# Hybrid decoder layer with grouped experts: expert slots padded to 32 rows instead of 128, four experts side by side in TensorE's column groups

## The reference, cut to what matters

```python
g_idx = jnp.argmax(g_logits, axis=-1)                      # 4 groups
top_v, top_i = lax.top_k(e_sel, 2)                         # 2 of the group's 4 experts
top_w = jax.nn.softmax(top_v, axis=-1) * p_g
combine = ...                                              # (tokens, 16), two entries per token
hg = jnp.einsum('td,edf->tef', t, w_e_gate)                # d 1024, f 256
hu = jnp.einsum('td,edf->tef', t, w_e_up)
act = jax.nn.silu(hg) * hu * combine[:, :, None]
return jnp.einsum('tef,efd->td', act, w_e_down)
```

## Time and profile before

| | |
|---|---|
| median of 3 runs | 1389.41 us |
| the profiled execution: span | 1389.9 us |
| TensorE matmul busy | 1280.3 us (92%) |
| VectorE busy | 1003.6 us (72%) |
| ScalarE busy | 742.2 us (53%) |
| mean granted TensorE clock | 0.967 |
| DMA moved | 229.41 MB, mean 165 GB/s |

### The profile page before, as it was taken

One profiled execution on the slowest core, in us unless ns is written; L12 is line 12 of the kernel. 1 busy time (PEld: TensorE's weight loads), 2 busy tenths in 40 slices (PEclk: granted clock), 3 DMA queues, 4 the chain that ended last, 5 costly groups with the idle time before them and its releaser, 6 DMA issues.

```text
span 1389.9 us, 25529 instructions
## 1 busy us (share of the span) xinstructions
PE 1280.3 (92%) x9230; PEld 1108.9 (80%) x9230; DVE 1003.6 (72%) x1532; ACT 742.2 (53%) x1323; POOL 129.9 (9%) x95
## 2 busy tenths in 40 slices
PE   4799999999999999999999996999389999999966
PEld 3598999999999999999999984777278887888832
DVE  2534457677585875858758667699879998999948
ACT  1445334454454544545545555422348998999825
POOL 1533200000000000000000000000011111111042
PEclk9899999999999999999999998999669999999988
DMA  9887433332342333322333243563177989655876
GB/s 321 261 277 243 134 106 102 88 84 84 88 117 66 89 95 94 115 59 82 107 97 102 84 138 91 163 199 152 76 280 254 372 292 376 205 184 182 285 258 200
DMA packets 210855, 229.41 MB, mean 165 GB/s; under 512 B 17942, under 2 KB 184666, under 8 KB 210619
## 3 DMA queue, kind: packets, MB, share of 16 engines
q1 hardware_dynamic: 195499, 173.33, 39.8%
q0 software_dynamic: 6976, 25.23, 5.4%
q10 hardware_dynamic: 8280, 29.51, 5.4%
HBM read 173.00 MB, written 46.79 MB: 158 GB/s over the span
## 4 chain that ended last, share of the span: by engine, by line
PE 72%; DVE 12%; DMA 4%; ACT 4%; SPq 3%; issue 3%; POOL 1%; ACTq 0%; DVEq 0%; POOLq 0%
PE AB L993 11%; PE AB L997 11%; PE AB L994 11%; PE S L918 6%; PE S L920 6%; PE S L919 6%; PE S L1093 4%; PE T L1119 3%; ACT F L1500 2%; DMA F<-in_b_ada 2%; PE OB L918 2%; PE OB L919 1%; PE OB L920 1%; SPq L624 1%; ACT R L1500 1%
## 5 line engine op out<-in xcount | busy, mean ns | idle before, releaser
L1500 ACT ACTIVATE R<-F 128x1024 fp32r<-128x1024 f32 (+4 forms) x306 | 292.4, 1003 | 74.2 <-DVE F L2084 39.6
L993 PE MATMUL AB<-R 128*128 128x344 f32 x960 | 314.9, 332 | 1.2 <-ACT F L1500 1.2
L994 PE MATMUL AB<-R 128*128 128x344 f32 x960 | 303.7, 320 | 0.0
L918 PE MATMUL S<-R 128*128 128x512 f32 x480 | 192.3, 401 | 2.0 <-ACT F L1500 1.6
L920 PE MATMUL S<-R 128*128 128x512 f32 x480 | 187.8, 391 | 0.0
L919 PE MATMUL S<-R 128*128 128x512 f32 x480 | 187.4, 390 | 0.0
L993 PEld LDWEIGHTS AB<-R 128*128 128x128 f32 x960 | 181.1, 189 | 4.8 <-issue 4.6
L994 PEld LDWEIGHTS AB<-R 128*128 128x128 f32 x960 | 181.4, 189 | 1.7 <-issue 1.7
L997 PE MATMUL AB<-R 128*128 128x344 f32 x960 | 171.6, 320 | 0.0
L1500 ACT ACTIVATE F<-AB 128x344 f32<-128x344 f32 (+3 forms) x129 | 59.0, 460 | 208.9 <-PE AB L997 193.5
L997 PEld LDWEIGHTS AB<-R 128*128 128x128 f32 x960 | 155.5, 188 | 0.0
(11 more groups left out here) (297 smaller groups left out, 2260.2 us busy)
## 6 DMA issues: line engine op xcount, KB each, us to landing
F<-in_w_ada SPq DMA_DIRECT2D x24, 1024.0 KB
F<-in_w_in SPq DMA_DIRECT2D x44, 512.0 KB, 4.2
F<-in_w_e_gate SPq DMA_DIRECT2D x16, 1024.0 KB, 5.9
F<-in_w_e_up SPq DMA_DIRECT2D x16, 1024.0 KB, 10.7
F<-in_w_e_down SPq DMA_DIRECT2D x16, 1024.0 KB, 10.9
y_d<-F ACTq DMA_DIRECT2D x32, 512.0 KB, 7.4
out<-F SPq DMA_DIRECT2D x24, 512.0 KB, 4.0
F<-F SPq DMA_DIRECT2D x192, 43.0 KB, 1.9
```

Of the source, the lines that this page charges most:

```text
L918: mm(out, w[0], m[1], start=start, stop=False)
L993: mm(bank[:, 0:PIECE], whl[b][0][:, k, :], x[1][:, k, :], start=(k == 0), stop=False)
L994: mm(bank[:, 0:PIECE], whl[b][0][:, k, :], x[0][:, k, :], start=False, stop=False)
L1500: return nc.scalar.activation(out, in_, func, **kw)
```

## The change

Slots are padded to 32 rows. 2064 pairs then take at most 80 subtiles of 32, laid out as four lanes of 20: lane j holds subtiles 20 j to 20 j + 19, in the order of the experts. A step n takes subtile n of each lane, four subtiles of up to four experts; the rows of lane j are rows 32 j to 32 j + 31 of the step's tile. There are 20 steps. The high and low splits are gone, of weights and of rows: products are native fp32 with the weights as they landed, each with a stationary operand of 32 columns whose output goes to 32 partitions of a bank. Each lane has one weight buffer (3 MB), and the tile `R` is also addressed as fp32 under the name `E`. VectorE copies the transposed rows and activations; ScalarE keeps SiLU and the eviction. All loops are unrolled.

```diff
+LANE = 32
+EXPERT_LANES = P // LANE
+STEPS = (2 * T + NE * (LANE - 1)) // LANE // EXPERT_LANES
+SUBTILES = STEPS * EXPERT_LANES
+SLOTS = STEPS * P
...
+            sp.wait_ge(wout_ready, NT + 1)
+            for q in range(2):
+                load_gate_up(0, 0, q)
+            load_down(0, 0)
...
+            sp.wait_ge(te_ready, 1)
+            first = [None] + [expert(j, 0) for j in range(1, EXPERT_LANES)]
+            for q in range(2):
+                for j in range(1, EXPERT_LANES):
+                    load_gate_up(first[j], j, q)
+            for j in range(1, EXPERT_LANES):
+                load_down(first[j], j)
             stage_end(sp, 1)
...
+            def next_gate_up(n, j, q):
+                e, prior = expert(j, n), expert(j, n - 1)
                 with sp.If(e != prior):
-                    load_gate_up(e, b)
+                    load_gate_up(e, j, q)
                 with sp.Else():
-                    sp.sem_inc(e_landed[b], 32)
+                    sp.sem_inc(gu_landed[j][q].sem, 32)
+
+            def next_down(n, j):
+                e, prior = expert(j, n), expert(j, n - 1)
                 with sp.If(e != prior):
-                    load_down(e, b)
+                    load_down(e, j)
                 with sp.Else():
-                    sp.sem_inc(d_landed[b], 16)
+                    sp.sem_inc(dn_landed[j].sem, 16)
...
+            for n in range(1, STEPS + 1):
+                for q in range(2):
+                    if n < STEPS:
+                        sp.wait_ge(gu_used, 2 * n - 1 + q)
+                        for j in range(EXPERT_LANES):
+                            next_gate_up(n, j, q)
+                if n >= 2:
+                    sp.wait_ge(dn_used, n - 1)
+                    for j in range(EXPERT_LANES):
+                        next_down(n - 1, j)
+                if 8 <= n < 8 + NT:
+                    t = n - 8
+                    sp.dma_start(x5[t], x1_d[t * P:(t + 1) * P, :]).then_inc(x5_landed[t // 4].sem, 16)
...
+        def gate_up(n):
+            b = n % 2
+            if n >= 2:
                 pe.wait_ge(av_done, n - 1)
             for q in range(2):
-                pe.wait_ge(g_hi, n * 4 + (2 * q + 2))
-                pe.wait_ge(g_lo, n * 2 + (q + 1))
-                pe.wait_ge(u_lo, n * 2 + (q + 1))
+                pe.wait_ge(xT_done_, 2 * n + q + 1)
+                for j in range(EXPERT_LANES):
+                    gu_landed[j][q].wait(pe, 32 * (n + 1))
                 for k in range(4 * q, 4 * q + 4):
-                    last = mm3(Sb[b], [x[:, k, :] for x in hg[b]], [w[:, k, :] for w in gu[b]], start=(k == 0), stop=(k == KC - 1))
-            last.then_inc(gu_used, 1)
+                    for j in range(EXPERT_LANES):
+                        rows = slice(LANE * j, LANE * j + LANE)
+                        last = mm(Sb[b][rows, :], xT[b][:, k, rows], gu[j][:, k, :], start=(k == 0), stop=(k == KC - 1), skip_group_check=True)
+                last.then_inc(gu_used, 1)
...
             for q in range(2):
                 for c in range(2):
-                    last = mm3(Sb[2 + q], [a[:, c, :] for a in aT], [w[:, c, 512 * q:512 * q + 512] for w in dn[b]],
-                               start=(c == 0), stop=(c == 1))
+                    for j in range(EXPERT_LANES):
+                        rows = slice(LANE * j, LANE * j + LANE)
+                        last = mm(Sb[2 + q][rows, :], aT[:, c, rows], dn[j][:, c, 512 * q:512 * q + 512],
+                                  start=(c == 0), stop=(c == 1), skip_group_check=True)
             last.then_inc(dn_used, 1)
...
+        turn_rows(0)
+        for n in range(STEPS):
+            if n + 1 < STEPS:
+                turn_rows(n + 1)
+            if n:
+                turn_act(n - 1)
+            gate_up(n)
+            if n == 0:
+                pe.wait_ge(ws_ready, 1)
...
+                pe.wait_ge(ws_copied, 1)
+            else:
+                down(n - 1)
+        turn_act(STEPS - 1)
+        down(STEPS - 1)
```

More of the change, by code:

```diff
@@ L78, in constants @@
     put("row", p[None, :])
-    put("start", P * np.arange(SLOT_TILES)[None, :])
+    put("start", LANE * np.arange(STEPS)[None, :])
+    put("first", LANE * p[:, None])
     valid = np.ones((P, NT + 1))
@@ L1393, in _ @@
                 n, rows = 9 * c + t, P if t < NT else NS
-                last = mm(OB[:, 0:SLOT_TILES], row_hot[0:rows, n, :], tile_tok[0:rows, n, :], start=(n == 0), stop=(n == 17))
+                last = mm(OB[:, 0:STEPS], row_hot[0:rows, n, :], tile_tok[0:rows, n, :], start=(n == 0), stop=(n == 17))
         last.then_inc(idx_ready, 1)
         stage_end(pe, 1)
[L1399 to L1413, removed]
+        def turn_rows(n):
+            b = n % 2
+            pe.wait_ge(xg_landed[b], 16 * (n // 2 + 1))
+            for c in range(2):
+                if n:
+                    pe.wait_ge(xT_done_, 2 * n - 1 + c)
+                for k in range(4 * c, 4 * c + 4):
+                    last = tr(TB[c][:, (k % 4) * P:(k % 4 + 1) * P], xg[b][:, k * P:(k + 1) * P], ident)
+                last.then_inc(xgT_ready, 1)
@@ L1429, in turn_act, with down @@
             last.then_inc(avT_ready, 1)
-        def down(n, b, later):
-            pe.wait_ge(avT_hi, n + 1)
-            pe.wait_ge(avT_lo, n + 1)
-            pe.wait_ge(dn_hi, n * 2 + 2)
-            pe.wait_ge(dn_lo, n * 2 + 2)
-            if later:
+        def down(n):
+            pe.wait_ge(avT_done, n + 1)
+            for j in range(EXPERT_LANES):
+                dn_landed[j].wait(pe, 16 * (n + 1))
+            if n:
                 pe.wait_ge(y_copied, n)
@@ L1442, in down @@
             last.then_inc(dn_used, 1)
-        def tile4(n, b, landed, before, more=True):
-            if more:
-                turn_rows(n + 1, 1 - b, landed, True)
-            if before >= 1:
-                turn_act(n - 1, before >= 2)
-            gate_up(n, b, before >= 2)
-            if before >= 1:
-                down(n - 1, 1 - b, before >= 2)
-        pe.wait_ge(ws_ready, 1)
-        for c in range(2):
-            for t in range(NT + 1):
-                n, rows = 9 * c + t, P if t < NT else NS
-                last = mm(PB[:, 0:SLOT_TILES], row_hot[0:rows, n, :].bitcast(F32), tile_w[0:rows, n, :], start=(n == 0), stop=(n == 17))
@@ L1459, in _ @@
-        last.then_inc(ws_ready, 1)
-        turn_rows(0, 0, 16, False)
-        tile4(0, 0, 16, 0)
-        tile4(1, 1, 32, 1)
-        with pe.Fori(1, SLOT_TILES // 2 - 1) as i:
-            for b in range(2):
-                tile4(i * 2 + b, b, i * 16 + 16 * (1 + b), 2)
-        tile4(SLOT_TILES - 2, 0, 16 * (SLOT_TILES // 2), 2)
-        tile4(SLOT_TILES - 1, 1, None, 2, more=False)
-        turn_act(SLOT_TILES - 1, True)
-        down(SLOT_TILES - 1, 1, True)
+        turn_rows(0)
+        for n in range(STEPS):
+            if n + 1 < STEPS:
+                turn_rows(n + 1)
+            if n:
+                turn_act(n - 1)
+            gate_up(n)
+            if n == 0:
+                pe.wait_ge(ws_ready, 1)
+                for c in range(2):
+                    for t in range(NT + 1):
+                        i, rows = 9 * c + t, P if t < NT else NS
+                        last = mm(PB[:, 0:STEPS], row_hot[0:rows, i, :].bitcast(F32), tile_w[0:rows, i, :], start=(i == 0), stop=(i == 17))
+                last.then_inc(ws_ready, 1)
+                pe.wait_ge(ws_copied, 1)
+            else:
+                down(n - 1)
@@ L1955, in _, with silu4 @@
         act.wait_ge(h2T_copied, 18)
-        def gate_up_hi(n, b, landed):
-            act.wait_ge(e_landed[b], landed)
-            for q in range(2):
-                k = slice(4 * q, 4 * q + 4)
-                act_(gu[b][0][:, k, 0:FF], raw_g[b][:, k, :]).then_inc(g_hi, 1)
-                act_(gu[b][0][:, k, FF:2 * FF], raw_u[b][:, k, :]).then_inc(g_hi, 1)
-        def silu4(n, b, later):
-            act.wait_ge(gu_used, n + 1)
-            if later:
+        stage_end(act, 1)
+        def silu4(n):
+            act.wait_ge(gu_used, 2 * n + 2)
+            if n:
@@ L1998, in tile4 @@
-        def tile4(n, b, i, before, more=True):
-            if more:
-                rows_hi(n + 1, 1 - b)
-            if before >= 1:
-                act_hi(n - 1, before >= 2)
-            if before >= 2:
-                rows_out(n - 2, b, i - 1, i * 16)
-            if more:
-                gate_up_hi(n + 1, 1 - b, i * 32 + 32 * (1 + b))
-            silu4(n, b, before >= 1)
-            down_hi(n, b, i * 16 + 16, before >= 2)
-        for b in range(2):
-            act.sem_inc(y_st[b], 16)
@@ L2028, in _ @@
-        rows_out(SLOT_TILES - 1, 1, HALF - 1, 16 * HALF)
+            if n == 0:
+                act.wait_ge(ws_copied, 1)
+            if n >= 2:
+                act.wait_ge(y_st[b], 16 * (n // 2))
+            act_(yv[b], S[:, 1024:2048], ACT.Copy, scale=wslot[:, n:n + 1]).then_inc(y_copied, 1)
+            act.wait_ge(y_copied, n + 1)
```

(61 more changed lines are left out.)

229 lines of the change are left out of this document (76 added, 153 removed).

## The result

The changed kernel takes 1506.61 us (median of 4 runs, 1505.63 to 1507.49) against 1391.32 us before (median of 4, 1388.94 to 1394.89): a ratio of 1.0816, 95% interval 1.0793 to 1.0839, or 115 us more. The forecast was 1477 us in a range of 1430 to 1545. The profiled execution has a span of 1504.8 us, 28 more than the sum, and a mean granted clock of 0.923 where it was 0.967.

The account below looks back on a forecast made before the run. SP was taken as the bound: 12 conditionals, 16.7 us a step against TensorE's 12.2. Start to 1051, SP's steps to 1397.5, last down to 1418.5, then the last part: 1477 us, range 1430 to 1545.

Parts of the forecast that it names:

- TensorE's step: One step's products and transposes on TensorE: 12 rounds of four at 0.90 us, transposes and switching, 12.2 us in all.
- A conditional: SP's branch on whether to load weights, with two reads of `te`: 1.39 us each, 228 in all.
- A step with no change: SP's 12 conditionals in a step where no lane changes expert: 16.7 us, more than TensorE's 12.2.
- A step with one change: A step in which one lane loads a new expert: 20 us; a change costs SP 2.8 us.
- The start: Up to step 1: barrier at about 1024, half 0 of step 0 ends at about 1035, of step 1 at 1051.
- SP in the steps: SP's work from 1051: 216 conditionals 300 us, changes of expert 42, `x5` loads 4.5, ending at 1397.5.
- Landings cost nothing: In the steps, 5.8 us for 1 MB of weights to land fit in TensorE's 7.5 us of slack, so cost nothing.
- down(19): The last step's down products on TensorE, after the last weights land: 3.6 us, ending at 1418.5.
- Rival 2: TensorE's clock falls after its waits; at 1.2 GHz a step is 24 us, the total 1565; full case chance 0.05.
- What would show it: Signs of being right: 456 reads, TensorE busy some 65%, waits ended by SP's raises, steps of 17 us, rounds 0.9 apart.
- Rival 1: TensorE stays the bound in the steps, so faster: 1336 us, up to 1345 where two lanes change at once; chance 0.10.
- Rival 3: The lanes run one after another on TensorE: 43.2 + 1.4 us a step, about 1965 us; chance 0.02.

Follow-up runs that it names:

- half-product kernel: Changed kernel with TensorE making only two of every four products of the contraction in each half of gate and up: 1496.32 us, one run.
- the kernel that reads once: Changed kernel with each entry of `te` read once per step and held in registers, 80 reads in the steps instead of 456: 1387.22 us.

## Why the prediction was right, and by how much its terms were off

The mechanism was right: SP's 228 conditionals bind, TensorE has slack, and the kernel is slower. The span is 28 us above the sum, and the terms stand like this.

- **TensorE's step**, 12.2 us: measured 11.68. Right. A round of four takes 6.89/8 = 0.86 us, less than the 0.90 of a single product in the earlier trace rows. Four products side by side thus cost no more than one. The Trainium skill ("TensorE: Matmul & The Clock Gate", Measured speedup vs the span model) gives 3.07 times for four row tiles; by that a round would be 1.17 us, an estimate from 4 x 0.90 us. For four column groups of native fp32 products with 512 columns the trace shows no such loss, and the measurement decides.
- **A conditional**, 1.39 us: 1.37 in the first four, a median of 1.36 over the steps. A step with no change, 16.7 us: measured 17.0 to 18.5. Right. A step with one change, 20 us: 19.8 to 22.5. The Trainium skill ("DMA: Bandwidth & Descriptors", Latency and other measured facts) has a floor of about 600 ns for a `tensor_load`; the trace shows 0.27 us for the load, and 0.505 us a read in all.
- **The start.** Half 0 of step 0 at 1035: SP, which waits for its end, reads on at 1037.3. Half 0 of step 1 at 1051: 1051.96. Right to 2 us. But the way there was another. The barrier ended at 1022, 2 us before my figure, and the sum had no term for the second gather, which waits for it: its rows are turned at 1030.06, 8 us later, and the first products wait for that. The slot weights behind the first block took 4.5 us (estimate 5 to 8), which gave most of that back.
- **SP in the steps: the term that was mis-sized.** From 1051 the sum had 346.5 us, to 1397.5; SP arrived at its wait for down(18) at 1418.3, 366 us. 1 us of the 20.8 is the later start. 17 us are reads that took longer than the median, up to 1.77 us, nearly all of them just behind one of ScalarE's stores of a result (below); 8 us are 22 short gaps; 2 us are the issues and `x5`, 48 against 46.5. The conditional itself, 1.36 and not 1.39 us, gives 7 back. The sum had no term for the reads and the gaps. The earlier trace rows had shown the maximum of 975 ns in the kernel before. I read only its median.
- **"Landings cost nothing"** held while SP binds, but at the end it is different: the wait of SP for down(18) took 7.9 us, not 3.6, as the last half of gate and up came late at step 19, and 1.7 us of it are that half's low clock (5.34 us for 3.64). From its end to the start of down(19) I had 13.6 us (5.6 and 8), and it took 13.2.
- **down(19)**, 3.6 us: 6.4 at the low clock after 12.85 us of idleness. Rival 2 in small: the clock fell to 0.86 in the steps and cost nothing there, by the half-product kernel, but it cost these 2.8 us and the 1.7 above at the end. The last part took 55.0 us from first gather to end where I had 54.2.
- 20.8 + 4.3 + 2.8 + 0.8, less 0.4 for that landing and 0.3 for the way to the last part (4.1 where I had 4.4), is the 28.
- **What would show it.** TensorE busy 65%: 68%. The step of 17 us: yes. "Waits ended by SP's raises and not by DMAs" was wrong as a sign: 27 of 34 waits bear a landing's name. With that, one of the prediction's own signs of being wrong, "TensorE waiting mainly for landings", came true by the names in the profile. The cause was as stated all the same, by the kernel that reads once; the sign was badly chosen.
- **Rival 1**, TensorE stays the bound, 1336 us: false for this kernel, but the number is what the kernel without re-reads and reloads gives, 1334.6. It meets it by two errors that nearly cancel: 20 steps take 234 us where the rival had 244, and the start some 7 us more than its 10. With the reloads it is 1387: my allowance of 9 us for changes of two lanes at once was far too small. It needs a second buffer, or the loads of the last step earlier. Neither was tried.
- **Rival 3**: its own terms (1023, 20 steps of 44.6 us, 59) add up to 1974, not 1965. Nothing hangs on it.

## What to carry to other kernels

When a change multiplies small decisions made at run time, price the sequencer that makes them as an engine of its own: count its instructions per step, and compare with the step of the busiest engine. And don't take the releaser of a wait for the bound: ask whether the queue that issues the transfers ever waits for the engine that waits for them. If it never does, as here for 366 us, suspect that queue of being the bound, whatever the waits are called, and take work off it to see.

## What the runs showed of the hardware

**Register reads become slow behind a store of another engine.** In the changed kernel, 32 of 459 reads take more than 400 ns, up to 1770. It is tempting to put this on the weight issue just ahead, and here is such a place: ScalarE's store of a result, SP's weight issue, and the reads behind both, 1562 ns and then 265.

```profile
1073.95 0.33 ACTq L1972 DMA_DIRECT2D y_d<-F  x1
...
1074.68 0.62 SPq L838 DMA_DIRECT2D E<-in_w_e_up  x1
...
L844 SPq TENSOR_LOAD <-te x2: 265/914/1562, 1075.5 to 1077.4; - x2
```

But behind the issues at 1083.80 and 1084.28, with no store near, the reads keep their time:

```profile
L844 SPq TENSOR_LOAD <-te x13: 263/266/274, 1082.4 to 1091.8; - x13
```

The same holds over the whole trace. 64 reads start within 1.5 us of a weight issue with no store in the last 5 us, and none takes more than 288 ns. Of the 32 slow ones, 30 start within 3.8 us behind ScalarE's store of 512 KB. In the kernel with no reloads in the steps there are still 29 slow reads, 27 of them 0.6 to 1.8 us behind a store, but none over 865 ns. So the slowness goes with the store, and where a weight load is on the way as well a read can take about twice as long. Up to 1343 us a gather of GpSimd's starts within 0.1 us of each store; behind the later stores, which have none beside them, reads are slow as well. No run moves the stores, so this stays a reading of when things happen.

**Short gaps in SP's stream.** Every 13 to 20 us, some 70 to 100 recorded instructions apart, SP stands still for 0.35 to 0.4 us between two instructions, at no fixed place of the step. The Trainium skill ("Runtime: NRT & Kernel Launch", Instruction fetch mechanics) tells of instructions fetched in blocks of 256 and of stalls where a taken branch leaves the pages held. The trace speaks for a fetch: after each of the 22 gaps, DMA queue 14, which the page of the profile calls `instruction`, starts a transfer of 8 KB, 1.0 to 4.0 us later. In the kernel without reloads it is 22 of 22 within 2.0 us, and in the loops of the kernel before there are no such gaps. The transfer starts when the gap is over, so the gap is not a wait for its data; what SP does in it stays open.

**A clock that costs nothing.** At a mean granted clock of 0.76 in its steps, the half-product kernel lost nothing by it there, and the changed kernel, at 0.86, lost 4.5 us by it at the end, in the last half of gate and up and in down(19). The clock of a stretch is a symptom of idleness there, and to be priced only where TensorE ends the wait of another.
